# Heads 8 to 15 of a hybrid decoder layer at three slots each, and the GLA state decay moved from GpSimd to ScalarE

## What is computed

```python
x = x + 0.5 * swiglu(rmsnorm(x, g_ffn1), w_ffn1_in, w_ffn1_out)
qa, ka, va, qg, kg, vg, rg, log_a = project(rmsnorm(x, g_mix), w_in, w_gate2, b_gate2)
o_att = softmax attention, 16 heads of 64, three dilated windows mixed by their denominators
S_t = diag(a_t) S_{t-1} + k_t^T v_t;  o_t = q_t S_t        # gated linear attention (GLA), 4 heads, 128 x 256 state
x = x + concat(rms(o_att) * g_att, rms(o_gla) * g_gla * silu(rg)) @ w_out
x = x + 0.5 * swiglu(rmsnorm(x, g_ffn2), w_ffn2_in, w_ffn2_out)
y = rmsnorm(x, g_final)
```

## Time and profile before

| | |
|---|---|
| median of 3 runs | 2107.7 us (2105.04 to 2108.38) |
| profiled execution | 2106.1 us, its span 2104.3 us |
| TensorE matmul busy | 2059.4 us, 98% |
| VectorE busy | 1176.0 us, 56% |
| ScalarE busy | 879.6 us, 42% |
| GpSimd busy | 153.1 us, 7% |
| granted TensorE clock, mean | 0.991 |

### The profile page before, as it was taken

The page is one execution under the profiler, slowest core; times in us unless marked ns, Lnnn a source line. Parts: engine busy times, 40 slices in busy tenths (PEclk is TensorE's granted clock), DMA queues, the critical chain, the costliest instruction groups (busy, mean ns, idle before and its releaser), DMA issues.

```text
span 2104.3 us, 40266 instructions
## 1 busy us (share of the span) xinstructions
PE 2059.4 (98%) x16603; PEld 2034.9 (97%) x16603; DVE 1176.0 (56%) x1231; ACT 879.6 (42%) x1013; POOL 153.1 (7%) x93
## 2 busy tenths in 40 slices
PE   8999999999999999999999899999999999999997
PEld 7999999999999999999988799999999999999997
DVE  6555555555444445665599877655555555544443
ACT  6443444444344435443346634443443334434332
POOL 0000000000000001005443550000000000000000
PEclk9999999999999999999999999999999999999998
DMA  6655565555555464548986465565566665665553
GB/s 206 188 179 179 166 193 180 179 179 180 180 181 180 161 201 136 160 131 271 328 264 207 152 194 169 171 193 181 179 180 180 179 180 164 191 183 177 180 174 109
DMA packets 200281, 387.52 MB, mean 184 GB/s; under 512 B 14458, under 2 KB 23364, under 8 KB 199924
## 3 DMA queue, kind: packets, MB, share of 16 engines
q1 hardware_dynamic: 193568, 377.80, 58.3%
q10 hardware_dynamic: 5956, 6.53, 0.9%
q0 software_dynamic: 656, 1.74, 0.2%
HBM read 376.91 MB, written 9.11 MB: 183 GB/s over the span
## 4 chain that ended last, share of the span: by engine, by line
PE 86%; DVE 7%; DMA 2%; ACT 2%; issue 2%; POOL 1%; ACTq 0%; SPq 0%; DVEq 0%
PE g L581 28%; PE g L582 28%; PE g L583 28%; DVE wl L1408 2%; ACT wh L1007 1%; DVE sm L1675 1%; DMA stream<-in_state_gla_dram 0%; DVE atl L1681 0%; DVE dif L1594 0%; DVE am L1617 0%; DVE sc_s L1692 0%; DMA xn<-in_x_prompt_dram 0%; PE g L850 0%; DMA raw<-in_w_out_dram 0%; DMA bcast<-rows_q 0%
## 5 line engine op out<-in xcount | busy, mean ns | idle before, releaser
L1408 DVE TENSOR_TENSOR wl<-raw,wh 128x1024 fp32r<-128x1024 f32 x658 | 814.9, 1248 | 762.2 <-ACT wh L1007 761.8
L1007 ACT ACTIVATE wh<-raw 128x1024 fp32r<-128x1024 f32 x658 | 689.7, 1055 | 866.4 <-PE g L583 829.3
L581 PE MATMUL g<-xh,wh 128*128 128x264 f32 x3584 | 1028.7, 287 | 5.1 <-DVE va L1561 2.6
L582 PE MATMUL g<-xl,wh 128*128 128x264 f32 x3584 | 1021.6, 285 | 0.0
L583 PE MATMUL g<-xh,wl 128*128 128x264 f32 x3584 | 1021.2, 285 | 0.0
L581 PEld LDWEIGHTS g<-xh,wh 128*128 128x128 f32 x3584 | 678.8, 189 | 10.8 <-issue 8.2
L582 PEld LDWEIGHTS g<-xl,wh 128*128 128x128 f32 x3584 | 677.5, 189 | 0.3
L583 PEld LDWEIGHTS g<-xh,wl 128*128 128x128 f32 x3584 | 676.1, 189 | 0.0
L581 PE MATMUL g<-uh,wh 128*128 128x264 f32 x1408 | 400.9, 285 | 0.0
L582 PE MATMUL g<-ul,wh 128*128 128x264 f32 x1408 | 400.6, 284 | 0.0
L583 PE MATMUL g<-uh,wl 128*128 128x264 f32 x1408 | 400.5, 284 | 0.0
(11 more groups left out here) (242 smaller groups left out, 1146.3 us busy)
## 6 DMA issues: line engine op xcount, KB each, us to landing
raw<-in_w_ffn_in_dram SPq DMA_DIRECT2D x352, 512.0 KB, 4.4
raw<-in_w_ffn_out_dram SPq DMA_DIRECT2D x176, 512.0 KB, 4.1
raw<-in_w_in_dram SPq DMA_DIRECT2D x96, 512.0 KB, 4.1
raw<-in_w_out_dram SPq DMA_DIRECT2D x32, 512.0 KB, 5.1
stream<-in_state_gla_dram SPq DMA_DIRECT2D x8, 512.0 KB, 7.4
bcast<-rows_v SPq DMA_DIRECT2D x8, 512.0 KB, 8.0
out_dram<-stream ACTq DMA_DIRECT2D x8, 512.0 KB, 6.8
stream<-in_cache_att_k_dram SPq DMA_DIRECT2D x8, 512.0 KB, 7.6
```

The lines of the kernel that those rows point to most:

```text
L581: pe.matmul(out(n), hi, a, start=first and k == 0, stop=False)
L582: pe.matmul(out(n), hi, b, start=False, stop=False)
L1007: act.activation(dst, src, ACT.Copy).then_inc(hi_done, 1)
L1408: dve.tensor_tensor(dst, src, h.bitcast(F32), ALU.subtract).then_inc(lo_done, 1)
```

## The change

`mixer_plan()` gives each of heads 8 to 15 three slots instead of two: they begin at slots 82, 85, 88, ... up to 103. The steps of a head keep their distances (`exp` + 1, `norm` + 2, and so on); `values` of head 15 moves from slot 101 to 108, `att_split` 7 from 103 to 110. A new step `decay` is put at slots 46, 48, ... 60, each one slot ahead of its `rec`, and is carried out by ScalarE in place of GpSimd's loop. In `after` all line numbers behind L1214 are larger by some 10 to 12.

```diff
--- before.py
+++ after.py
@@ -156,6 +156,7 @@
 
     s += 9
     for b in range(TS):
+        put(s + 2 * b - 1, "decay", b)
         put(s + 2 * b, "rec", b)
         put(s + 2 * b + 2, "rec_out", b)
         put(max(s + 2 * b + SP_LAG, s + SP_LAG) if b < 4 else s + 2 * b + SP_LAG - 1, "load_state", b)
@@ -175,13 +176,14 @@
             put(by_buf["qa", 4] + 2, "nat", ("qa", 2, grp))
         for i in range(H_ATT // 2):
             h = H_ATT // 2 * grp + i
-            put(s + 2 * i, "score", h)
-            put(s + 2 * i + 2, "norm", h)
-            put(s + 2 * i + 1, "exp", h)
-            put(s + 2 * i + 3, "probs_t", h)
-            put(s + 2 * i + 5, "values", h)
+            at = s + (3 if grp else 2) * i
+            put(at, "score", h)
+            put(at + 2, "norm", h)
+            put(at + 1, "exp", h)
+            put(at + 3, "probs_t", h)
+            put(at + 5, "values", h)
             if h % 2:
-                put(s + 2 * i + 7, "att_split", h // 2)
+                put(at + 7, "att_split", h // 2)
 
     s = max(rec_end - 4 + SP_AHEAD, by_buf["qa", 4] + 2 + SP_AHEAD) - SP_LAG + 1
     for b in range(TS):
@@ -1212,6 +1214,14 @@
                 act.activation(sfin[:, 2 * pair:2 * pair + 2, :].rearrange("p a b -> p (a b)"), bank,
                                ACT.Copy).then_inc(done, 1)
 
+            def decay(b):
+                act.wait_ge(a_exp, 1)
+                act.wait_ge(st_in[b % 4], 16 * (b // 4 + 1))
+                for h in range(H_GLA):
+                    st = stream[:, b % 4, h * DV:(h + 1) * DV]
+                    a = act.activation(st, st, ACT.Copy, scale=a_s[:, h, b:b + 1])
+                a.then_inc(decayed, 1)
+
             def rec_out(b):
                 bank, done = filled(act, "rec_out", b)
                 act.activation(og[:, :, TP + b], bank[:, 0:2 * H_GLA], ACT.Copy).then_inc(done, 1)
@@ -1328,6 +1338,8 @@
                         kd_nat(arg)
                     elif step == "state":
                         state_(arg)
+                    elif step == "decay":
+                        decay(arg)
                     elif step == "rec_out":
                         rec_out(arg)
                     elif step == "exp":
@@ -1900,14 +1912,6 @@
             pool.dma_start(mult[:, :], c_mult).then_inc(attc_in, 16)
             pool.dma_start(mask[:, :], c_mask).then_inc(attc_in, 16)
 
-            pool.wait_ge(a_exp, 1)
-            for b in range(TS):
-                pool.wait_ge(st_in[b % 4], 16 * (b // 4 + 1))
-                for h in range(H_GLA):
-                    st = stream[:, b % 4, h * DV:(h + 1) * DV]
-                    a = pool.tensor_scalar(st, st, a_s[:, h, b:b + 1], None, ALU.mult)
-                a.then_inc(decayed, 1)
-
             for b in range(TS):
                 pool.wait_ge(bc_in[b % 2], 16 * (TS // 2 + b // 2 + 1))
                 for t in range(2):
```

## The result

The changed kernel takes 2122.0 us (median of 5 runs, 2117.8 to 2125.4), the kernel before 2107.7 on the same chip: 1.0064 times as long, with a 95% interval of 1.0045 to 1.0083. It is slower by some 13.5 us (9.5 to 17.5) by this ratio, and by 14.3 by the two medians, where 6 us of gain were forecast. The profiled execution took 2122.0 us.

The account below looks back on a forecast made before the run. TensorE was taken as the bound, with 19.3 us lost to waits and low clock in heads 8 to 15. Terms (a) to (f) left 13.3 lost, so a gain of 6.0 and 2101.7 us; range 2098 to 2105.

Parts of the forecast that it names:

- (a): Head 8's transposes: score 9 now comes after them, TensorE arrives 1.0 us earlier, wait grows from 0.45 to 1.5 us.
- (b): Tiles of the second rg block, slot 89: a wait of 2.0 us where 1.5 stood.
- (c): Slot 90, bank 2: TensorE waits 0.5 us for ScalarE's read between values 9 and gla_mean 1.
- (d): Head 11, slot 94, takes head 12's place: VectorE late, wait 3.8 us and 1.4 of low clock behind it.
- (e): Tiles of the last rg block, slot 97: less VectorE work in slot 96, so 1.9 us become 0.6.
- (f): Head 13, slot 100, takes head 15's place: wait 2.8 us plus 0.7 of clock; the wait of 5.1 goes.
- (h): Behind slot 100, heads 14 and 15: no loss there, 0 us, and 0 for the tail.
- (g): ScalarE's table loads: eleven become eight, taking 3.8 us off ScalarE, counted inside (d) to (f).
- A: Rival: nothing new waits, (d) and (f) vanish, VectorE on time; 8.7 us more gain, 2093.0 us; chance 0.14.
- B: Rival: VectorE paces the whole stretch, so order does not matter; gain 0.3, 2107.4 us; chance 0.24.
- C: Rival: slower, norms 13 to 15 held beside GpSimd's multiplies; 2118.3 us, or 2111.6 with two held; chance 0.13.
- D: Rival: the decay stops ScalarE's splits while a state is on its way, up to +13, 2108 to 2120; chance 0.04.

Follow-up runs that it names:

- e_spacing: Kernel before with heads 8 to 15 at three slots each, decay left on GpSimd; 2118.7 us.
- e_decay: Changed kernel with all heads put back to two slots, decay kept on ScalarE; 2104.7 us.
- e_svalue_after: Changed kernel with the 8 s_value steps (16 one-column matmuls each) one slot later; 2110.4 us.
- e_svalue_before: Kernel before with the 8 s_value steps one slot later; 2114.2 us.
- e_offset_after: Changed kernel with heads 8 to 15 starting one slot later, still three slots each; 2106.5 us.
- pool cuts: GpSimd's weighting of the cached values cut to 64 of 1024 columns: kernel before 2093.3 us, changed kernel 2098.9 us.
- the shifts: Changed kernel with steps one slot later: transposes of heads 8 to 15 2107.4 us, s_value 2110.4, whole heads 8 to 15 2106.5.
- e_late_after: Changed kernel with only the transposes of heads 8 to 15 one slot later; 2107.4 us.
- e_fill_after: Changed kernel with unused filler matmuls ahead of the transposes of head 11 (26) and head 13 (48); 2118.6 us.
- e_pool_before: Kernel before with GpSimd's weighting of the cached values cut to 64 of 1024 columns; 2093.3 us.
- e_pool_sv_after: Changed kernel with GpSimd's weighting cut to 64 of 1024 columns and the s_value steps one slot later; 2101.8 us.

## Why the prediction was wrong

**The stretch and its two kinds of wait: right.** The loss was sought where it is: slots 81 to 111 hold 11.7 of the 15.9 us between the two profiled executions, and 15.4 of the 18.3 between the kernel before and e_spacing.

**The decay, 0 us: right**, down to 13.5 us busy and 0.3 us of wait, with e_decay at -2.3 (-5.5 to 0.8).

**The waits (a) to (e): right in place and nearly in size.**

| step | forecast | trace after |
|---|---|---|
| (a) head 8 | 1.5 | 1.5 |
| (b) tiles, slot 89 | 2.0 | 2.2 |
| (c) bank 2 | 0.5 | 0.5 |
| (d) head 11 | 3.8 + clock 1.4 | 3.3 + clock 5.1 |
| (e) tiles, slot 97 (all its idle time) | 0.6 | 1.2 |
| (f) head 13 | 2.8 + clock 0.7 | 6.1 + clock 6.8 |
| (h) behind slot 100 | 0 | 1.1 + clock 5.1 |
| a wait of L828 for ScalarE, slot 87 | not seen | 1.1 |
| sum | 13.3 | 34.0 |

(The sum after counts 1.8 us twice, for idle time at half clock. Its 12.1 us of waits of L806 also pass the 9 that the prediction had named as a sign of being wrong.)

**The clock terms are the step that failed.** "I charge 1.4 to a wait of 3 to 4 us and less to a shorter one, a choice": 2.1 us in all, where 17.0 stand in the trace. They make 15 of the 20.7 us by which the sum is too small (13 without what is counted twice), and the forecast was 20.3 too low. The sum was lopsided even by its own rows: the 19.3 us lost before hold all 6.9 us of clock, and the 13.3 after only the 2.1 that were charged to two waits. The small matmuls of the sample values, which the prediction names as the other cause of low clock, went in at nothing, without a reason. With the other 4.8 us left in, the gain would have been 1.2 and not 6.0. I took the price from the kernel before as if it belonged to a wait. It belongs to the wait and to what TensorE does behind it, and the change altered that: my own step (a) had noticed that the score now stands behind the transposes, but not that `s_value` does too in every second slot of a head's. The exchange of signs in e_svalue_after and e_svalue_before, and e_offset_after, which keeps the spacing and has none of the loss, speak for this as what made the changed kernel slow; each of them moves VectorE against GpSimd too, so its share is not measured.

**(f) was short by 3.3 us in the wait itself.** (Its own terms, 7 less 2.9 and 1, give 3.1 and not 2.8.) The mechanism was right, and "3.2 of them lengthening" was carried over for the old row only; att_split 5 and the second subtract were priced unhindered, "0.9" and "1.2", and took 4.3 and 3.35. What is put beside GpSimd's pair of multiplies is to be priced at its slow length. The rule that I had quoted from the Trainium skill (SBUF — State Buffer, Who interferes with whom) names VectorE instructions with two SBUF inputs as those that contend with a GpSimd instruction that reads SBUF, and these are such. The pool cuts agree with it: 32 us of VectorE's busy time go with GpSimd's columns.

**(h) "I take 0" failed**: half clock in slots 102, 106 and 108, 10.2 us in all, with a single wait of 1.1.

**(g) was right** in the count of loads, eight; what their 3.8 us are worth was not tried alone.

**The rivals.** A (nothing waits) is out. B put 2107.4 on the ground that VectorE paces the stretch, and would have been right for most of the variants: six orders came out within 2 us of before, five of them with their longest wait at block rg's tiles. C had the sign, and its share of the cause: lengthened VectorE work beside the multiplies. But it asked for heads 13, 14 and 15 to be held; head 14 was not, head 15 by 1.1 us, and the missing 10 us were clock. D is out.

**How the two causes share the loss.** By the pool cuts, with VectorE quick, the changed order costs 5 us over the old one and not 13.5, so by the medians more than half of it needs GpSimd's hold on VectorE. By the shifts, parting the thin work from the waiting transposes takes all of it away, with VectorE's busy time hardly changed in e_late_after (127.8 us) and 7 to 10 us lower in the other two. My reading, which the runs allow but do not prove, is that the two multiply rather than add: the lengthening makes a long wait, and behind it the clock stays low through the thin work, which costs another 5 us at each (half of 10.2 and of 13.7, less the idle part). In e_fill_after some of what a quicker clock gave was spent on waiting for the tiles of block rg. What stays open is the size of the clock's part, since every way tried to hold it up also moved TensorE against VectorE or added work of its own, and why no slot of e_pool_before falls to half clock, though slots 94 and 96 hold an `s_value` beside a score there too.

## What to carry to other kernels

Price a wait of TensorE together with what it runs next: behind both long waits here the clock stood at half through the transposes, the score and the one-column matmuls, and came back only inside the full chunk after them. A sum of losses after must hold every kind of loss that the sum before holds. A filler put in the place of a wait is to be checked against the moment at which the wait would have ended. When steps are respaced, list which of them come to share a slot: three slots a head against two slots a sample made heads 11, 13 and 15 coincide here, and a shift by one slot undid the loss. An instruction that is moved beside another engine's long instructions, where its neighbours are seen to last longer, is priced at the slow length of such neighbours, not at its own elsewhere.

## What the hardware showed that was not expected

TensorE's granted clock fell to half without any idle time before it, behind 3.1 us of unbroken small work (7 instructions of 128 to 256 columns and 16 of one column) in slot 97 of e_pool_sv_after, and without idle time in three more slots of it. And cutting GpSimd's multiplies to a sixteenth of their columns, though GpSimd is busy 7% of the time, is worth 15.2 us of 2107.7 in the kernel before: more than any order of the heads that was tried.
